# Routing of a mixture-of-experts block: fixed experts for the first 32 blocks, block 0 gathered by one-hot products, tables built behind it

## What is computed

```python
def moe_ffn(xn, ...):                        # xn = rms_norm(h, norm_ffn_g)
    logits = xn @ w_router + b_router        # 512 x 32
    top_val, top_idx = lax.top_k(logits, 4)
    gates = jax.nn.softmax(top_val, axis=-1)
    ...
    h = x_pad[toks]                          # the rows of one expert
    gate = jnp.minimum(h @ w_gate[e] + b_gate[e], 7.0)
    up = jnp.clip(h @ w_up[e] + b_up[e], -7.0, 7.0)
    return ((up + 1.0) * gate * sigmoid(1.702 * gate)) @ w_down[e] + b_down[e]
```

## Time and profile before

| | us |
|---|---|
| median of 3 runs | 1633.84 |
| lowest, highest | 1630.9, 1635.97 |
| the profiled execution, its own time | 1628.32 |
| its span | 1626.5 |
| TensorE busy, share of the span | 94% |
| VectorE, ScalarE, GpSimd busy | 81%, 67%, 15% |
| bytes moved | 490.22 MB |

### The profile page before, as it was taken

One profiled execution on the slowest core, in us unless ns is written; L12 is line 12 of the kernel. 1 busy time (PEld: TensorE's weight loads), 2 busy tenths in 40 slices (PEclk: granted clock), 3 DMA queues, 4 the chain that ended last, 5 costly groups with the idle time before them and its releaser, 6 DMA issues.

```text
span 1626.5 us, 29442 instructions
## 1 busy us (share of the span) xinstructions
PE 1525.0 (94%) x10381; PEld 1258.3 (77%) x10381; DVE 1311.5 (81%) x1445; ACT 1090.1 (67%) x1302; POOL 244.6 (15%) x249
## 2 busy tenths in 40 slices
PE   7999978889769999999999999999999999999990
PEld 6877768877658888888888888888888888888870
DVE  4247455545579999999999999999999999999977
ACT  4245431113447888788888888888888888888851
POOL 6000321101100311122211100010101000101112
PEclk9999999999879999999999999999999999999995
DMA  6311110002569999999999999999999999999946
GB/s 227 93 59 40 40 40 3 4 5 80 216 229 368 420 411 406 414 409 411 408 406 416 406 407 405 408 406 403 408 404 408 405 400 407 412 400 407 405 196 265
DMA packets 88202, 490.22 MB, mean 301 GB/s; under 512 B 13952, under 2 KB 15148, under 8 KB 38220
## 3 DMA queue, kind: packets, MB, share of 16 engines
q1 hardware_dynamic: 78636, 472.52, 73.0%
q0 software_dynamic: 9360, 16.80, 2.7%
q10 hardware_dynamic: 144, 0.00, 0.0%
HBM read 485.60 MB, written 20.97 MB: 311 GB/s over the span
## 4 chain that ended last, share of the span: by engine, by line
PE 76%; DVE 9%; DMA 7%; issue 5%; ACT 2%; DVEq 0%; POOL 0%; POOLq 0%; ACTq 0%; SPq 0%
PE banks L359 62%; PE banks L1633 5%; DMA expert_w_raw<-in_moe_w_down_dram 4%; DVE expert_w_lo L300 3%; ACT expert_w_hi L295 1%; DVE residual L1615 1%; PE banks L1726 1%; PE banks L1896 1%; PE banks L1893 1%; DMA expert_w_raw<-in_moe_w_gate_dram 1%; DMA expert_w_raw<-in_moe_w_up_dram 1%; PE banks L1878 1%; PE banks L1710 1%; PE banks L1831 1%; DVE up_act L1089 1%
## 5 line engine op out<-in xcount | busy, mean ns | idle before, releaser
L300 DVE TENSOR_TENSOR expert_w_lo<-expert_w_raw,expert_w_hi 128x1024 fp32r<-128x1024 f32 x768 | 893.7, 1220 | 72.6 <-ACT expert_w_hi L295 65.1
L295 ACT ACTIVATE expert_w_hi<-expert_w_raw 128x1024 fp32r<-128x1024 f32 x768 | 765.0, 1055 | 112.5 <-DMA expert_w_raw<-in_moe_w_up_dram 38.1
L359 PE MATMUL banks<-expert_w_hi,x_block_T_hi 128*128 128x512 f32 x992 | 389.3, 392 | 0.0
L359 PE MATMUL banks<-expert_w_lo,x_block_T_hi 128*128 128x512 f32 x992 | 386.9, 390 | 0.0
L359 PE MATMUL banks<-expert_w_hi,x_block_T_lo 128*128 128x512 f32 x992 | 386.1, 389 | 0.0
L359 PE MATMUL banks<-expert_w_hi,h_block_T_hi 128*128 128x512 f32 x544 | 217.6, 400 | 7.8 <-DVE h_block_T_lo L1075 3.6
L359 PEld LDWEIGHTS banks<-expert_w_lo,x_block_T_hi 128*128 128x128 f32 x992 | 186.2, 188 | 39.4
L359 PEld LDWEIGHTS banks<-expert_w_hi,x_block_T_lo 128*128 128x128 f32 x992 | 186.4, 188 | 38.1
L359 PEld LDWEIGHTS banks<-expert_w_hi,x_block_T_hi 128*128 128x128 f32 x992 | 186.4, 188 | 37.8
L359 PE MATMUL banks<-expert_w_lo,h_block_T_hi 128*128 128x512 f32 x544 | 213.7, 393 | 0.0
L359 PE MATMUL banks<-expert_w_hi,h_block_T_lo 128*128 128x512 f32 x544 | 213.4, 392 | 0.0
(11 more groups left out here) (353 smaller groups left out, 1755.1 us busy)
## 6 DMA issues: line engine op xcount, KB each, us to landing
expert_w_raw<-in_moe_w_gate_dram SPq DMA_DIRECT2D x128, 1024.0 KB, 12.5
expert_w_raw<-in_moe_w_up_dram SPq DMA_DIRECT2D x128, 1024.0 KB, 13.1
expert_w_raw<-in_moe_w_down_dram SPq DMA_DIRECT2D x128, 1024.0 KB, 13.0
gate_bias_rows<-in_moe_b_gate_dram SPq DMA_DIRECT2D x32, 512.0 KB, 11.4
up_bias_rows<-in_moe_b_up_dram SPq DMA_DIRECT2D x32, 512.0 KB
w_raw<-in_w_in_dram SPq DMA_DIRECT2D x24, 512.0 KB, 3.7
expert_w_raw<-y_pair_rows SPq DMA_DIRECT2D x6, 1024.0 KB, 10.1
residual<-in_x_dram SPq DMA_DIRECT2D x8, 512.0 KB, 5.0
```

The costliest lines, as they stand in the source:

```text
L295: act.activation(self.hi[:, k % self.nhl, 0:width], self.raw[:, k % self.nraw, 0:width], ACT.Copy)\
L300: dve.tensor_tensor(self.lo[:, k % self.nhl, 0:width], self.raw[:, k % self.nraw, 0:width], self.hi[:, k % self.nhl, 0:width].bitcast(F32) ...
L359: last = pe.matmul(o, lhs, rhs, start=start and t == 0, stop=stop and t == 2, skip_group_check=preset)
```

## The change

- The first 32 blocks have fixed experts: block j is expert j's first block; what an expert has above 128 rows goes into blocks 32 and on. SyncE takes the expert from the loop index, and each engine reads the number of blocks after the loop over the first 32 (`tables_ok` moved behind it). Bias rows are fetched for each block as before.
- The router works on rows that aren't normed: the norm's gain is multiplied into the router weights once, early on, and the inverse root of the mean square is applied to the logits. Transposes and logits of a tile stand between the output units of the next (`out_units`). Squares go to SBUF instead of PSUM.
- Ranks are computed tile by tile (`ranks`, `places`), and give two one-hot tables, of the rows of blocks 0 and 1. Block 0's transposed rows are products of the normed rows with the first (`block0_x`), without gather or transposes. Block 1's token numbers come from the second (`block1_tokens`), behind block 0's first chunk.
- The place sums (`dest`) are made on VectorE between low parts; the tables behind them (`ohR`, `dcmp`, `rhsv`) move to POOL, the slot sums to TensorE behind chunk 5 of block 1, the index tables to VectorE behind low part 8 of block 1. Bank pairs of the four token tiles are exchanged (`PAIR_OF`).

The diff, cut to its core:

```diff
+    param(NT[:, 0:KT], t_in["norm_ffn_g"][0].rearrange("(p k) -> p k", k=KT))
...
-    def block_loads(i):
-        e = expert(i)
+    def block_loads(i, e, e_before):
         sp.wait_ge(S("gate_bias"), i)
         sp.dma_start(BG[:, :], bias_rows("moe_b_gate", e)).then_inc(S("gate_bias_in"), 16)
         loads(i, 0, wg_v, e)
         sp.wait_ge(S("up_bias"), i)
         sp.dma_start(BU[:, :], bias_rows("moe_b_up", e)).then_inc(S("up_bias_in"), 16)
         loads(i, 8, wu_v, e)
-        loads(i, 16, wd_v, expert(i - 1))
-    block_loads(1)
+        loads(i, 16, wd_v, e_before)
+    block_loads(1, 1, 0)
...
-    pool.wait_ge(S("xn2_stored"), 16 * TT)
-    pool.wait_ge(S("x2T_ps"), TT)
...
+    pool.wait_ge(S("slots_ok"), 1)
+    pool.wait_ge(S("xn2_stored"), 16 * TT)
     gather(1, 0)
...
+    def floor_of(out, value, scale, shift):
+        ch.link(pool.tensor_scalar(out, value, scale, shift, ALU.mult, ALU.add))
+        ch.link(pool.tensor_scalar(out, out, MAGIC, None, ALU.add))
+        ch.link(pool.tensor_scalar(out, out, -MAGIC, None, ALU.add))
+    pool.wait_ge(S("places_ok"), 1)
+    floor_of(dover[:, :], dest[:, :], 1.0 / OVER, (-ROW0 - (OVER - 1) / 2) / OVER)
+    ch.link(pool.tensor_scalar(dmore[:, :], dover[:, :], -OVER, None, ALU.mult))
+    ch.link(pool.tensor_tensor(dest[:, :], dest[:, :], dmore[:, :], ALU.add))
+    floor_of(dfull[:, :], dest[:, :], 1.0 / P, (-ROW0 - (P - 1) / 2) / P)
+    ch.link(pool.tensor_scalar(dmore[:, :], dfull[:, :], -float(P), None, ALU.mult))
+    ch.link(pool.tensor_tensor(destr[:, :], dest[:, :], dmore[:, :], ALU.add))
...
+    ch.link(pool.tensor_tensor(dover[:, :], dover[:, :], dfull[:, :], ALU.add))
+    ch.link(pool.tensor_scalar(dover[:, :], dover[:, :], float(NE - 1), None, ALU.add))
+    ch.link(pool.tensor_tensor(by_tile[1], by_tile[1], e_of, ALU.subtract))
+    ch.link(pool.tensor_scalar(dmore[:, :], dfull[:, :], 1.0, None, ALU.min))
+    ch.link(pool.tensor_tensor(dover[:, :], dover[:, :], dmore[:, :], ALU.mult))
+    ch.link(pool.tensor_tensor(by_tile[0], by_tile[1], e_of, ALU.add))
+    for m in range(NP):
+        pool.tensor_scalar(ohR[:, m, :], iotaR[:, :], destr[:, m:m + 1], None, ALU.is_equal)
+    for m in range(NP):
+        ins = pool.tensor_scalar(dcmp[:, m, :], iotaB[:, :], destb[:, m:m + 1], None, ALU.is_equal)
+    ch.link(ins)
+    pool.tensor_scalar(rhsv[:, 0], dcmp[:, :, :], iotaP[:, 2:3], None, ALU.mult).then_inc(S("pairs_ok"), 1)
+    for t in range(1, TT):
+        ms = slice(TOPK * t, TOPK * t + TOPK)
+        ins = pool.tensor_scalar(rhsv[:, 1, ms], dcmp[:, ms], float(P * TOPK * t), None, ALU.mult)
+    ins.then_inc(S("pairs_ok"), 1)
+    for k in range(1, TOPK):
+        ins = pool.tensor_scalar(rhsv[:, 2, k::TOPK], dcmp[:, k::TOPK], float(k + 1), None, ALU.mult)
+    ins.then_inc(S("pairs_ok"), 1)
     def block_pool(i):
         first = isinstance(i, int)
-        pool.wait_ge(S("xT_ps"), i + 1)
+        pool.wait_ge(S("xT_ps"), i + 2)
+        if first:
+            pool.wait_ge(S("slots_ok"), 3)
...
+    def block0_hi(b):
+        act.wait_ge(S("xT_ps"), b + 1)
+        act.activation(hbh[:, 4 * b:4 * b + 4, :].rearrange("p k t -> p (k t)"), bank[4 + b], ACT.Copy)\
+            .then_inc(S("xT_hi"), 1)
     mixed_square(0)
+    x2T_act(0)
+    first_hi(0, 1)
     mixed_square(1)
-    x2T_act(0)
+    gate_exp(0)
+    x2T_act(1)
+    first_hi(1, 2)
     mixed_square(2)
-    x2T_act(1)
-    gate_exp(0)
+    gate_exp(1)
+    x2T_act(2)
+    first_hi(2, 4)
+    gate_exp(2)
     mixed_square(3)
-    x2T_act(2)
-    first_hi(0, 2)
-    gate_exp(1)
-    gate_exp(2)
     x2T_act(3)
-    first_hi(2, 4)
-    gate_exp(3)
-    first_hi(4, 8)
     act.wait_ge(S("banks_swept"), 1)
     gate_bias(act, 0)
-    xT_hi(act, 0)
-    act.wait_ge(S("tables_ok"), 1)
-    nb = act.value_load(n_blk[0:1, 0:1], min_val=NE, max_val=NB - 1)
-    last_blk = act.value_load(n_blk[0:1, 1:2], min_val=NE - 1, max_val=NB - 2)
+    first_hi(4, 6)
+    gate_exp(3)
+    block0_hi(0)
+    block0_hi(1)
+    first_hi(6, 8)
+    act.wait_ge(S("banks_swept"), 2)
     up_bias(act, 0)
-    first_hi(8, 11)
+    first_hi(8, 13)
     xT_hi(act, 1)
-    first_hi(11, 14)
+    first_hi(13, 14)
     swish(act, 0, MOE0 + 8)
     first_hi(14, 16)
     block_act(act, 1)
...
+        hT_lo(dve, 0)
+        slot_tables()
+        lo(8, 21)
+        up_part(dve, 1, base_of(1) + 16)
+        lo(21, 23)
+        xT_lo(dve, 2)
+        lo(23, 24)
+        return
...
+    def places(tt):
+        dve.wait_ge(S("rank_ps"), tt + 1)
+        ch.link(dve.scalar_tensor_tensor(slotm[:, tt, :], MB[:, tt, :], ROW0, bank[2 * PAIR_OF[tt] + 1][:, 0:NE],
+                                         ALU.mult, ALU.add))
+        dve.tensor_scalar(oh0[:, tt, :], iotaR[:, :], slotm[:, tt, 0:1], None, ALU.is_equal)
+        dve.tensor_scalar(oh1[:, tt, :], iotaR[:, :], slotm[:, tt, 1:2], None, ALU.is_equal)\
+            .then_inc(S("rows_ok"), 1)
...
+    mixed_add(3, 0)
     normed(2)
-    for f in range(2):
-        mixed_add(3, f)
-    x2T_dve(2)
-    route(1)
+    first_lo(0, 2)
+    route(2)
+    first_lo(2, 3)
+    places(2)
+    mixed_add(3, 1)
+    x2T_dve(3)
+    mean_square(3)
     normed(3)
-    route(2)
-    x2T_dve(3)
-    first_lo(0, 1)
     route(3)
+    places(3)
     dve.wait_ge(S("gate_exp"), TT)
     ch.link(dve.reciprocal(rgs[:, :], gsum[:, :]))
...
+    first_lo(3, 4)
+    block0_lo(0)
+    block0_lo(1)
+    dve.wait_ge(S("xn2_stored"), 16 * TT)
+    first_lo(4, 5)
+    dve.wait_ge(S("slots_ps"), 1)
+    ch.link(dve.tensor_scalar(skip1[:, :], bank[7][:, 0:1], 0.0, SKIP, ALU.is_equal, ALU.mult))
+    dve.scalar_tensor_tensor(idx_x[:, 1:2], bank[7][:, 0:1], -1.0, skip1[:, :], ALU.add, ALU.add)\
+        .then_inc(S("slots_ok"), 1)
+    first_lo(5, 7)
+    dve.wait_ge(S("rank_ps"), TT + 1)
+    cnt = bank[6][:, 0:NE]
     for b in range(4):
...
+    ch.link(dve.tensor_tensor(over[:, :], bend[:, :], iota32[:, :], ALU.subtract))
+    ch.link(dve.tensor_scalar(ecmp[:, :], over[0:NBT, :], iotaP[0:NBT, 1:2], None, ALU.is_le))
+    ch.link(dve.tensor_tensor(over[:, :], over[:, :], nbl[:, :], ALU.subtract))
+    first_lo(7, 8)
+    ch.link(dve.scalar_tensor_tensor(rank[:, :, :], bc(over[:, :], [P, TT, NE], 1), OVER, slotm[:, :, :],
+                                     ALU.mult, ALU.add))
     ch.link(dve.tensor_tensor(dtmp[:, :, :, :], OH[:, :, :, :],
                               rank[:, :, :].unsqueeze(2).to_broadcast([P, TT, TOPK, NE]), ALU.mult))
...
-    dve.tensor_tensor(ohR[:, :, :], bc(destr[:, :], [P, NP, P], 2), bc(iotaR[:, :], [P, NP, P], 1), ALU.is_equal)
-    ch.link(dve.tensor_tensor(dcmp[:, :, :], bc(destb[:, :], [P, NP, NBT], 2), bc(iotaB[:, :], [P, NP, NBT], 1),
-                              ALU.is_equal))
-    for v in range(3):
-        ins = dve.tensor_tensor(rhsv[:, v], dcmp[:, :, :], bc(pair_ids[:, v, :], [P, NP, NBT], 2), ALU.mult)
-    ins.then_inc(S("pairs_ok"), 1)
...
+    dve.reduce_sum(dest[:, :], dtmp[:, :, :, :].rearrange("p t k e -> p (t k) e"), AXX)\
+        .then_inc(S("places_ok"), 1)
+    first_lo(8, 10)
     ch.link(dve.reduce_sum(bef[:, :], ecmp[:, :], AXX))
-    dve.tensor_scalar(bef[:, :], bef[:, :], float(NE - 1), None, ALU.min).then_inc(S("pairs_ok"), 1)
-    first_lo(1, 3)
-    dve.wait_ge(S("slots_ps"), 1)
...
-    dve.sem_inc(S("slots_ok"), 1)
-    dve.wait_ge(S("experts_ps"), 1)
-    dve.tensor_copy(blk_exp[0:1, :], bank[4][0:1, 0:NBT])
+    ch.link(dve.tensor_scalar(bef[:, :], bef[:, :], float(NE - 1), None, ALU.min))
+    dve.tensor_tensor(bef[:, :], bef[:, :], iotaP[0:NBT, 3:4], ALU.add).then_inc(S("places_ok"), 1)
     dve.tensor_copy(n_blk[:, 0:1], bend[:, NE - 1:NE])
-    dve.tensor_scalar(n_blk[:, 1:2], bend[:, NE - 1:NE], -1.0, None, ALU.add)\
-        .then_inc(S("tables_ok"), 1)
+    dve.tensor_scalar(n_blk[:, 1:2], bend[:, NE - 1:NE], -1.0, None, ALU.add)
+    first_lo(10, 15)
+    xT_lo(dve, 1)
+    first_lo(15, 16)
...
+    def slot_tables():
+        dve.wait_ge(S("slots_ps"), 3)
+        sp_ = bank[4][:, 0:2 * NBT].rearrange("p (a b) -> p a b", a=2)
+        ch.link(dve.tensor_scalar(skipv[:, :], sp_[:, 1, :], 0.0, SKIP, ALU.is_equal, ALU.mult))
+        dve.scalar_tensor_tensor(idx_x[:, 2:NBT], sp_[:, 0, 2:NBT], 0.25, skipv[:, 2:NBT], ALU.mult, ALU.add)\
+            .then_inc(S("slots_ok"), 1)
+        ch.link(dve.tensor_tensor(slotv[:, :], sp_[:, 1, :], skipv[:, :], ALU.add))
+        dve.scalar_tensor_tensor(idx_y[:, :], sp_[:, 0, :], -1.0, slotv[:, :], ALU.add, ALU.add)\
+            .then_inc(S("slots_ok"), 1)
+        dve.wait_ge(S("slots_ps"), 4)
+        dve.tensor_copy(blk_exp[0:1, :], bank[5][0:1, 0:NBT]).then_inc(S("tables_ok"), 1)
...
-    x2_flip(3)
+    def ranks(tt):
+        pe.wait_ge(S("member_ok"), tt + 1)
+        for t2 in range(tt + 1):
+            last = pe.matmul(bank[2 * PAIR_OF[tt] + 1][:, 0:NE], (triu if t2 == tt else ones_b)[:, :], MB[:, t2, :],
+                             start=t2 == 0, stop=t2 == tt)
```

(69 more changed lines are left out.)

268 lines of the change are left out of this document (135 added, 133 removed).

## The result

The changed kernel takes 1651.8 us at the median of four runs (1647.1 to 1654.7), against 1632.6 us; the ratio is 1.0118, with a 95% interval of 1.0095 to 1.0141. So it is slower by 19 us, where the forecast was 7 us faster. The profiled run took 1654.7 us with a span of 1652.9, 26.4 above that of before.

A forecast was written before the change was run, and what follows sets the result against it. The prediction took the transfer stream, full from 505 us on, to set the end; low part 28 coming 7 us earlier gave 1628.3 - 7 = 1621.3 us profiled, 1626.8 at the median, range 1619 to 1638.

The forecast's parts named there:

- only what moves that point moves the end: Expert stage: transfer stream full from 505 us on, at 34.85 us a block; only moving that point moves the end.
- low part 28: VectorE work in block 1 whose end releases the last of block 1's loads; forecast 498 against 505.2, 7 us earlier.
- Last use of the output weights: Before routing: last output unit ends at 434.9, not 427.1; stream restarts 7.8 us later, capping the gain at 14.7 us.
- Products: Block 0's rows by 32 f32 products, 64 passes at 0.125 us, 8 us; block 0 starts at 448.5, 19 us earlier.
- rival 3: Front eats it: 1.2 GHz products or later members put block 0 and place sums 7 us back; 1631 to 1635; chance 0.20.
- POOL's 55 operations: Table building on POOL from 459.1: 16.3 us alone, slowed beside VectorE's low parts, ending near 491.5.
- one operation for each 1.2 us: POOL's table building: beside VectorE's low parts, POOL gets one operation through per 1.2 us, 15 of 55 by 489.
- rival 2: POOL late: tables end at 511, VectorE stops in the slot tables, +12 us, 1646; chance 0.14.
- The join: Slot sums, slot tables and four low parts behind POOL's last value: low part 28 ends 6.2 to 6.5 us after it.
- With no cost: gather 2 is issued at 496, needed 10 us later: Second gather, around block 1: issued at 496, needed 10 us later, so costed at nothing.
- The value loads moved behind the loop: Reads of the block counts, moved behind the loop over blocks: costed at nothing.
- The sum: Whole kernel: 1628.3 less 7 gives 1621.3 us on the profiled clock, 1626.8 at the median.

The follow-up runs named there:

- no_copy: Changed kernel, second gather reading its row numbers from the table without POOL's one-element copy: 1651.7 us, ratio 1.0115.
- order: Changed kernel, wait for tile 2's memberships behind the last output unit, routing of tile 2 ahead of two low parts: 1651.6 us, ratio 1.0122.
- contig: Changed kernel, normed rows stored with feature groups side by side, so the products' stationary operand is contiguous: 1645.1 us, ratio 1.0074.
- tables_dve: Changed kernel, the 55 table operations back on VectorE behind low part 9, each one-hot as one operation: 1645.5 us, ratio 1.0084.
- both: Changed kernel, tables back on VectorE and no index copy in front of the second gather: 1644.9 us, ratio 1.0064.
- tail: Changed kernel, TensorE's wait for the tables and two value loads ahead of the block loop again: 1649.2 us, ratio 1.0120.
- gap: Changed kernel, no index copy, VectorE waiting behind the slot tables until POOL has issued the second gather: 1649.2 us, ratio 1.0122.
- gap_tail: Changed kernel, no index copy, VectorE waiting for the second gather's issue, TensorE's value loads ahead of the loop: 1644.0 us, ratio 1.0075.
- best3: Changed kernel, tables on VectorE behind low part 12, early slot sums, contiguous operand, new order, high parts 13-15 and value loads ahead: 1626.8 us, ratio 0.9982.

## Why the prediction was wrong

**What sets the end.** That the stream sets it from the middle on holds: from 1000 to 1500 us the share is 1.00, the gate bias comes every 34.52 us up to 1026 and every 34.97 on average after. What failed is "only what moves that point moves the end". I had the stream full from low part 28 on without a break. But the ring is finite: TensorE stood idle from 529.5 to 536.8 for the held gather, and the window 520 to 560 is 0.90. In the table the way from low part 28 to block 31 costs 6.1 to 7.8 us over the kernel before in the five other kernels with a held gather (no_copy, order, contig, tables_dve, both; "tail" has 6.9 too), and -0.6 to 2.8 in the seven without.

**Last use of the output weights**, 434.9: measured 437.78, or 435.1 by the marker. Right, and idle, as "order" shows.

**Products**, 0.125 us a pass: measured 0.24 (7.72 us for 32 at the full clock). This term of the sum was mis-sized by 7 us. My nearest row was one of 512 columns with a contiguous operand; the layout of the stationary operand, not the number of columns, made the price, and with neighbouring elements it is about 0.13 (8.5 us of loads for 64). The first expert matmul came at 457.7 instead of 448.5, the place sums at 467.7 instead of 459.1. Of rival 3 the size came, but the cause was not the clock, which was 1.00 from 450 to 458.

**POOL's 55 operations**, 32.4 us from the place sums: measured 42.9. This is the second mis-sized term. The single one-hots show what was wrong with it, one with VectorE idle and one beside five low parts in a row:

```profile
479.08 0.62 POOL L719 TENSOR_SCALAR onehot_row<-iota_rows,dest_row 128x128 bf16<-128x128 f32 x1
...
482.84 2.38 POOL L719 TENSOR_SCALAR onehot_row<-iota_rows,dest_row 128x128 bf16<-128x128 f32 x1
```

A one-hot costs 0.59 to 0.62 us where VectorE leaves POOL alone, and I had 0.30; the compares cost 0.38 instead of 0.23, the seven pair values 6.7 us instead of 3.5, the linked ones about 0.33 with their wait instead of 0.27. By these rows I estimate the chain alone at 27.4 us, against the 16.3 of the prediction: 11 us, the whole of the miss. The time added by VectorE is then 15.5 us, against 16.1. So what it added in all came out right, and the rule behind it did not: "one operation for each 1.2 us" beside low parts is the mean of the one-hots (1.17), but inside the run of five each of them took 2.38 us, two low parts, and one linked operation took 3.55 beside three.

With the late start of 8.7 us this puts POOL's end at 510.7, not 491.5. That is **rival 2**, with its end at 511 and its +12 us at low part 28 (12.0 by the profile's clock, 9.3 by the common one); I had given it 0.14, and the forecast 0.50. Its condition came true for the one-hots (0.59 where it asks for 0.55), not for the compares. That its 511 was met to the microsecond is luck: it had no late start in it, and 40 operations left at 489 where 31 were left. Its evidence, that POOL has no row of this operation, was in the text, and I priced the operations by additions of other shapes.

**The join**: right as a mechanism, low part 28 ends 6.4 us behind POOL's pair values (517.1 against 510.7); in the kernel before it ends at 504.9, not 505.2.

**"With no cost: gather 2 is issued at 496, needed 10 us later."** Wrong. It is issued at the head of a run of 13 low parts that I had in my own rows, beside an operation of POOL that I had priced at 1.2 us a piece next to a low part. What I had not asked is what happens when the low parts leave no gap: here POOL waited for the whole run, twice, with a copy and with an issue. The Trainium skill (SBUF — State Buffer, Summary: rules for kernel authors) says that beside a VectorE instruction with two SBUF inputs a POOL instruction that reads SBUF, if it is the second to issue, is blocked until the first finishes; for the copy the rows agree and show more, since it was held through 13 instructions in turn. The price at block 31 is 5.7 us (no_copy to gap) or 4.3 (tail to gap_tail), and 5.2 in the medians of the second pair.

**"The value loads moved behind the loop."** Wrong for TensorE, right for SyncE: 3.1 us of idle time ahead of the last transposes, of which the loads are half. In the kernel before they stood behind block 0, with the whole loop behind them in which TensorE has time to spare.

**The sum** then reads, by the common clock, +9.3 for low part 28 instead of -7, about +7 for the way from there to block 31 (4 to 6 of it the held gather) and +3 for the tail: 19, which is the medians' difference. The front did get earlier: block 0's first matmul by 12.6 us (457.72 less 2.7, against 467.62), not 19, and none of it reached the end.

**What stays open.** In the changed kernel's own profile the way from low part 28 to block 31 costs 11.2 us, 4 more than in its relatives; one profile cannot say whether this is scatter. In best3 2.8 us of the 6.9 are lost on the same way with no held gather. The 1.5 us that TensorE stands idle behind the loop is not explained. And of two POOL instructions beside an unbroken run of low parts, one was held to the end (14.76 us) and another came in after two (2.38 us); no run tells why.
